# MLA head loop: the next head's first key/value tile (T0) multiplied ahead of the key transposes (kp) instead of behind them

## The chip, the cores and the metric

The kernel runs on one core of a Trainium2 chip. The metric is the device time of one execution in microseconds. A profiled execution of the kernel before took 2205.33 us; the trace of it spans 2203.3 us.

## The reference

One inference step of a two-layer encoder: a forgetting-attention layer (FoX), then a multi-head latent attention layer (MLA), for a prompt of 512 tokens and for 64 new tokens that follow 512 cached ones. The change lies in the MLA attention. With c the normalised latent (512 wide) of all tokens and w_ukv its up-projection, each of 16 heads computes

```
kv     = c @ w_ukv[head]                        # 256 wide: 128 key columns, 128 value columns
kn, v  = rms_norm(kv[:, :128]) * g_kn, kv[:, 128:]
logits = (qn @ kn.T + qr @ kr.T) * MLA_SCALE    # nope part + rotary part (kr shared by the heads)
p      = softmax(where(kpos // 64 <= qpos // 64, logits, -1e30))
o      = (p @ v) * silu(gate)
```

and then y = x + o @ w_out. Everything is fp32. The kernel splits each operand of a matmul into a rounded high part and a low part (fp32r) and adds three products, hi*hi, hi*lo and lo*hi.

## The kernel before

The MLA attention is `block_f` (line 2514), with the helpers of class `MlaHead`. It is one software pipeline over heads: one pass of the loop does the attention of head g = h - 1 and, between its steps, the key/value projection of head h. Passes run for h = 0 (no g), h = 1 to 14 as seven turns of a hardware loop with two passes each, h = 15, and at last one with g = 15 alone, in which the output projection takes the place of the tiles.

The order of a pass is a list of names written out by hand, `ORDER` (line 2109). Each of the engines walks the same list and emits what that name means for it; all waits are semaphores between engines. An engine's queue is in order, so an instruction that waits holds all behind it. The names:

- **T0 to T7**: TensorE multiplies one tile of 128 tokens with the head's weights (`pe_tile`, line 2251): 12 matmuls of 256 columns, two tiles to a PSUM bank, banks 0 to 3. T0 to T3 are prompt tokens, T4 to T7 cached ones. T8 (8 matmuls, bank 4) is for the new tokens. T0 waits for the head's split weights and, in `v_lo`, until VectorE has taken the values of the head before out of bank 0. After T1, T3, T5 and T7 ScalarE squares the keys of the two tiles (`act_keys`), VectorE turns the sums into variances (`dve_sums`), GpSimd takes the root, and VectorE writes the normalised keys to f_k (`dve_keys`) in two halves: the first (prompt keys) at the name "sb" of the same pass, the second (cached and new keys) at "kp" of the next.
- **kp, ka, new**: TensorE transposes the prompt keys, the cached keys, and the new tokens' queries and keys (`pe_job`, line 2276). ScalarE copies the result to the high part and VectorE subtracts to get the low part (f_kphi, f_kplo; f_knhi, f_knlo).
- **s3 to s0, sa, sb**: scores of four prompt blocks (s3 is the longest, 512 columns) and of the new tokens. VectorE masks and takes the maximum (f_nm), ScalarE the exponential (f_p; f_pn for the new tokens).
- **p3 to p0, pn**: transposes of the probabilities, split as above (f_pt3hi, f_pt3lo, ...). **on, o**: probabilities times values. **g**: transposes of the gate, which VectorE has scaled by the reciprocal of the softmax sum (`dve_scale_gate`). **ont**: transpose of the new tokens' output. **qr, qn**: transposes of the next head's queries, split into f_qr, f_qnhi and f_qnlo.

The jobs (names without T) take turns in three PSUM banks, 5, 6 and 7, in the order of the list. So `wait_operands` (line 2202) makes each job wait until the third job before it has been taken out of its bank, besides its own inputs: kp shares its bank with qn, s2, s0, p3, p1 and g; s3 with o and new; p1 waits for f_pt3lo. s3 to s0 need kp, qr and qn to be split, sa and sb need ka and new.

At the name "kp" the other engines do more than the job. ScalarE, after f_kphi, waits for the second half of the keys, takes the values out of banks 2, 3 and 4 (f_v_past) and rounds the next head's weights (f_whi). VectorE, after f_kplo, writes the second half of the keys and then the values' low parts. The names T0, T2 and T6 mean nothing to them. `FIRST`, the order of the pass h = 0, is made from `ORDER`; `FINAL`, the order of the last pass, is a list of its own.

GpSimd, besides the roots, does leftovers of the stage before in the first passes (scaling and rotating the queries of the last heads, e_q and e_rt) and parts of the output projection's splits in the last. SP issues the loads: the next queries once "new" has run, the next gate once "ont" has run.

Of the kernel before, what the change touches and what calls it, by code (L numbers as in the profile page):

```python
# [2101 lines left out]
class MlaHead:  # L2102
# [3 lines left out]

    ORDER = ["kp", "T0", "T1", "s3", "ka", "T2", "s2", "new", "T3", "s1", "s0", "T8", "sa", "sb", "T4",
             "p3", "T5", "pn", "p2", "p1", "T6", "on", "p0", "g", "T7", "ont", "qr", "qn", "o"]  # L2110
    NEXT = ("qr", "qn")
    FIRST = [n for a in ORDER if a not in ("qr", "qn") for n in ((a, "qr", "qn") if a == "T5" else (a,))]
    FINAL = ["kp", (0, 0), (0, 1), "s3", "ka", (0, 2), "s2", "new", (0, 3), "s1", "s0", (0, 4), "sa", "sb", (1, 0), (1, 1),
# [3 lines left out]
    SPLIT_AT = {"T2": 0, "T3": 1, "T7": 2, (0, 1): 3, (1, 3): 4, (2, 3): 5, (3, 3): 6}  # L2117
    JOBS = [n for n in ORDER if n[0] != "T"]
    SPLITS = ["kp", "ka", "new", "p3", "pn", "p2", "p1", "p0", "qr", "qn"]
# [64 lines left out]
    def order(self, h):  # L2184
        return self.FINAL if h is None else self.FIRST if isinstance(h, int) and h == 0 else self.ORDER

# [709 lines left out]
```

How the kernel before makes its waits and increments, by code:

```python
    def wait(self, eng, step, k):  # L70
        v = (step * self.per + k + self.credit + self.ahead) * self.unit
        if not isinstance(v, int) or v > 0:
            eng.wait_ge(self.sem, v)
# [186 lines left out]
    def pe(self, eng, part=slice(None)):  # L261
        for i, b, ks, s, prev in self.jobs()[part]:
            if prev is not None:
                eng.wait_ge(self.lo_out.sem, prev + 1)
            for j, k in enumerate(ks):
                if s:
                    op = eng.transpose(self.c.bank[b][:, j * NEW:(j + 1) * NEW],
                                       self.src[0:NEW, SM, k * P:(k + 1) * P], self.ident[0:NEW, 0:NEW])
                else:
                    for t in range(NT):
                        op = eng.transpose(self.c.bank[b][:, t * P:(t + 1) * P],
                                           self.src[:, t, k * P:(k + 1) * P], self.ident[:, :])
            op.then_inc(self.turned.sem, 1)
# [1 line left out]
    def act(self, eng, part=slice(None)):  # L275
        for i, b, ks, s, _ in self.jobs()[part]:
            src, hi, lo = self.views(b, ks, s)
            eng.wait_ge(self.turned.sem, i + 1)
            eng.activation(hi, src, ACT.Copy).then_inc(self.hi_out.sem, 1)
# [1 line left out]
    def dve(self, eng, part=slice(None)):  # L281
        for i, b, ks, s, _ in self.jobs()[part]:
            src, hi, lo = self.views(b, ks, s)
            eng.wait_ge(self.hi_out.sem, i + 1)
            eng.tensor_tensor(lo, src, hi.bitcast(F32), ALU.subtract).then_inc(self.lo_out.sem, 1)
```

## Time and profile before

| | |
|---|---|
| median of 3 runs | 2205.38 us (2205.34 to 2206.18) |
| profiled execution, its time | 2205.33 us |
| its span in the trace | 2203.3 us |
| TensorE, matmul / weight load | 99% / 85% of the span |
| VectorE, ScalarE, GpSimd | 51%, 43%, 10% |
| MLA head loop, passes with kp and tiles | 1612.2 to 1985.3 us, 15 passes |
| a steady pass | 24.77 us |

Line 2270 is the tiles' matmul, 2299 the transposes of kp and ka, 2305 and 2307 the scores, 2328 the product o, 2337 the gate's transposes. A row of a timeline has the start in us, the duration in us, the engine (PE is TensorE's matmul, PEld its weight load, DVE VectorE, ACT ScalarE, POOL GpSimd), the line, the operation, output<-inputs, sizes, how many are merged, and in brackets the idle time of that engine just before it and what ended it. Matmuls overlap in the trace: the next one starts while the record of the one before is still open, so the time that one takes of the stream is the distance between starts.

### The profile page before, as it was taken

The page shows a single profiled execution, that of the slowest core. Times are in us where ns is not written, and L with a number is a line of the kernel's source. Part 1 is how long each engine was busy: PE and PEld are TensorE (multiplying, and loading weights), DVE is VectorE, ACT ScalarE, POOL GpSimd, SP SyncE. Part 2 cuts the span into 40 slices and gives each one's busy share as a digit, 9 for nine tenths or more (in the row PEclk, how much of TensorE's full clock was granted, in tenths as well). Part 3 has the DMA queues.
Part 4 walks back from the last instruction along what each step waited for, and adds up shares of the span by engine and source line. Part 5 has one row for each costly group of instructions (what it writes and reads, how often), then busy time and mean ns, then how long its engine had stood idle before and what let it go on. Part 6 is the DMA issues. An engine that isn't in the chain of part 4 may idle for free. (4 is left out here: it accounts for less than half of the span.)

```text
span 2203.3 us, 33500 instructions
## 1 busy us (share of the span) xinstructions
PE 2187.6 (99%) x11665; PEld 1872.6 (85%) x11665; DVE 1119.6 (51%) x2676; ACT 955.7 (43%) x2242; POOL 229.5 (10%) x248
## 2 busy tenths in 40 slices
PE   9999999999999999999999999999999999999999
PEld 6888888888888888888888988888899999998887
DVE  6645554445454545555223344454477777775232
ACT  5444444434444444453223433344366666664111
POOL 0100000000000000000000001332150100021000
PEclk9999999999999999999999999999999999999999
DMA  5333332333333334333432332433431212122542
GB/s 180 104 102 111 101 101 92 106 106 101 98 90 103 110 101 101 102 103 115 156 119 82 108 103 80 148 115 133 129 103 48 60 51 57 48 60 71 172 128 92
DMA packets 127443, 225.27 MB, mean 102 GB/s; under 512 B 21216, under 2 KB 70624, under 8 KB 127248
## 3 DMA queue, kind: packets, MB, share of 16 engines
q1 hardware_dynamic: 127376, 224.36, 33.2%
q8 instruction: 45, 0.74, 0.1%
q14 instruction: 22, 0.18, 0.0%
HBM read 191.42 MB, written 32.89 MB: 102 GB/s over the span
## 5 line engine op out<-in xcount | busy, mean ns | idle before, releaser
L213 PE MATMUL bank<-b_whi,x_hi 128*128 128x512 f32 x1016 | 401.8, 395 | 0.8 <-DVE b_wlo L196 0.8
L213 PE MATMUL bank<-b_whi,x_lo 128*128 128x512 f32 x1016 | 396.5, 390 | 0.0
L213 PE MATMUL bank<-b_wlo,x_hi 128*128 128x512 f32 x1016 | 396.5, 390 | 0.0
L196 DVE SCALAR_TENSOR_TENSOR b_wlo<-b_raw,g_fox,b_whi 128x512 fp32r<-128x512 f32 x254 | 179.1, 746 | 137.4 <-ACT b_whi L183 136.9
L183 ACT ACTIVATE b_whi<-b_raw,g_fox 128x512 fp32r<-128x512 f32 x254 | 169.1, 714 | 152.7 <-PE bank L213 134.8
L213 PEld LDWEIGHTS bank<-b_whi,x_lo 128*128 128x128 f32 x1016 | 190.7, 188 | 41.0
L213 PEld LDWEIGHTS bank<-b_whi,x_hi 128*128 128x128 f32 x1016 | 190.9, 188 | 37.3 <-DVE b_wlo L196 1.1
L213 PEld LDWEIGHTS bank<-b_wlo,x_hi 128*128 128x128 f32 x1016 | 190.9, 188 | 35.3
L213 PE MATMUL bank<-m_whi,x_hi 128*128 128x512 f32 x320 | 125.0, 391 | 0.0
L213 PE MATMUL bank<-m_wlo,x_hi 128*128 128x512 f32 x320 | 124.6, 389 | 0.0
L213 PE MATMUL bank<-m_whi,x_lo 128*128 128x512 f32 x320 | 124.6, 389 | 0.0
L196 DVE SCALAR_TENSOR_TENSOR m_wlo<-m_raw,g_mla,m_whi 128x512 fp32r<-128x512 f32 x80 | 61.7, 812 | 95.7 <-ACT m_whi L183 95.6
L183 ACT ACTIVATE m_whi<-m_raw,g_mla 128x512 fp32r<-128x512 f32 x80 | 53.4, 716 | 124.8 <-PE bank L213 124.8
L1048 POOL TENSOR_TENSOR b_decay<-b_decay,mask_fox 128x128 f32<-128x128 f32 x64 | 27.8, 466 | 738.1 <-DMA b_decay_new<-decay 738.1
L213 PE MATMUL bank<-c_whi,x_hi 128*128 128x512 f32 x256 | 100.7, 393 | 1.2 <-DVE x L1445 1.2
L213 PE MATMUL bank<-b_whi,x_smp 128*128 128x512 f32 x254 | 101.8, 401 | 0.0
L213 PE MATMUL bank<-g_whi,g_ohi 128*128 128x512 f32 x256 | 100.4, 392 | 0.0
L213 PE MATMUL bank<-c_whi,x_lo 128*128 128x512 f32 x256 | 99.8, 390 | 0.0
L213 PE MATMUL bank<-c_wlo,x_hi 128*128 128x512 f32 x256 | 99.7, 390 | 0.0
L213 PE MATMUL bank<-g_whi,g_olo 128*128 128x512 f32 x256 | 99.7, 389 | 0.0
L213 PE MATMUL bank<-g_wlo,g_ohi 128*128 128x512 f32 x256 | 99.7, 389 | 0.0
L192 DVE TENSOR_TENSOR g_wlo<-g_raw,g_whi 128x1024 fp32r<-128x1024 f32 x32 | 39.1, 1223 | 118.9 <-ACT g_whi L179 118.9
(506 smaller groups left out, 5102.2 us busy)
## 6 DMA issues: line engine op xcount, KB each, us to landing
b_raw<-w_fox SPq DMA_DIRECT2D x127, 512.0 KB, 3.5
m_raw<-w_mla SPq DMA_DIRECT2D x40, 512.0 KB, 3.5
c_raw<-w_out SPq DMA_DIRECT2D x32, 512.0 KB, 3.5
g_raw<-w_out SPq DMA_DIRECT2D x32, 512.0 KB, 3.5
f_raw<-w_ukv SPq DMA_DIRECT2D x16, 512.0 KB, 3.6
queries<-e_q SPq DMA_DIRECT2D x16, 480.0 KB, 3.8
e_raw<-w_uq SPq DMA_DIRECT2D x32, 192.0 KB, 2.6
f_qa<-queries SPq DMA_DIRECT2D x16, 320.0 KB, 3.7
```

The lines of the kernel that those rows point to most:

```text
L183: op = eng.activation(hi[:, k, :], raw[:, k, :], ACT.Copy, scale=self.gain[:, K:K + 1])
L192: op = eng.tensor_tensor(lo[:], raw[:], hi32, ALU.subtract)
L196: op = eng.scalar_tensor_tensor(lo[:, k, :], raw[:, k, :], self.gain[:, K:K + 1], hi32[:, k, :], ALU.mult, ALU.subtract)
L213: op = eng.matmul(out, a, w[:, k, :], start=(first and k == 0 and i == 0), stop=(last and k == self.kk - 1 and i == len(pairs) - 1))
L1048: pool.tensor_tensor(x, x, K.mask_fox[:], ALU.add).then_inc(H.decay_masked.sem, 1)
```

## The change

In `ORDER` the first two names change places. The list is read by all engines, but only TensorE does something at T0, so only its order changes: the 12 matmuls of T0 stand ahead of the four transposes of kp in each pass with a g and an h. `FIRST` is derived from `ORDER` (in the pass h = 0 kp does nothing on TensorE), `FINAL` stays. Which bank each job uses, and what it waits for, is unchanged.

```diff
-    ORDER = ["kp", "T0", "T1", "s3", "ka", "T2", "s2", "new", "T3", "s1", "s0", "T8", "sa", "sb", "T4",
+    ORDER = ["T0", "kp", "T1", "s3", "ka", "T2", "s2", "new", "T3", "s1", "s0", "T8", "sa", "sb", "T4",
              "p3", "T5", "pn", "p2", "p1", "T6", "on", "p0", "g", "T7", "ont", "qr", "qn", "o"]
```

## Rows read from the trace of the kernel before

**Rows 1.** By windows: span, busy time (count) of each engine, PEclk, DMA.
```profile
1711.74:1736.51 24.77, 24.52 (x190) 23.02 (x190) 18.11 (x60) 15.22 (x56) 2.17 (x2) 1.00 0.18 53
...
1959.31:1985.27 25.96, 24.95 (x190) 23.04 (x190) 19.50 (x60) 18.19 (x62) 10.12 (x10) 1.00 0.27 80
```
**Rows 2.** Waits of TensorE: us in total, times, longest.
```profile
PE bank L2299 <- DVE f_qnlo L2438: 3.6, 15, 0.3
```
**Rows 3.** Timeline of TensorE, a steady pass, from o to new.
```profile
1711.21 0.27 PE L2328 MATMUL bank<-f_pt3hi,f_v_own 128*128 128x128 f32 x1
1711.74 0.65 PE L2299 MATMUL bank<-ident,f_k 128*128 128x128 f32 x4 [0.26 <-DVE f_qnlo L2438]
1712.15 0.36 PE L2270 MATMUL bank<-f_whi,c_hi 128*128 128x256 f32 x1
...
1715.11 0.40 PE L2305 MATMUL bank<-f_kphi,f_qnhi 128*128 128x512 f32 x1
...
1716.27 0.60 PE L2299 MATMUL bank<-ident,f_k 128*128 128x128 f32 x4
...
1719.10 0.43 PE L84 MATMUL bank<-ident,f_qa 64*128 64x64 f32 x2
```
**Rows 4.** Timeline of VectorE, the same pass.
```profile
1710.92 0.69 DVE L2438 TENSOR_TENSOR f_qnlo<-bank,f_qnhi 128x512 fp32r<-128x512 f32 x1
...
1713.06 0.69 DVE L2438 TENSOR_TENSOR f_kplo<-bank,f_kphi 128x512 fp32r<-128x512 f32 x1 [0.65 <-ACT f_kphi L2358]
...
1716.16 0.27 DVE L2511 TENSOR_TENSOR f_v_past<-f_kv_new,f_v_past 64x128 fp32r<-64x128 f32 x1
```
**Rows 5.** Timeline of ScalarE, the same pass.
```profile
1712.43 0.60 ACT L2358 ACTIVATE f_kphi<-bank 128x512 fp32r<-128x512 f32 x1 [1.81 <-PE bank L2299]
1715.07 0.66 ACT L2429 ACTIVATE f_v_past<-bank 128x256 fp32r<-128x256 f32 x2 [2.04 <-DVE f_k L2505]
...
1717.38 0.69 ACT L2383 ACTIVATE f_p<-bank,f_nm 128x512 f32<-128x512 f32 x1
...
1725.66 0.50 ACT L2378 ACTIVATE f_pn<-bank,f_nm 64x288 f32<-64x288 f32 x1 [0.77 <-DVE f_nm L2449]
```
**Rows 6.** Timelines of VectorE and TensorE, the same pass, from s1 to g.
```profile
1721.96 0.11 DVE L2453 MEMSET bank<- 64x64 f32 x1 [0.23 <-PE bank L2307]
...
1727.82 0.29 DVE L2438 TENSOR_TENSOR f_pt3lo<-bank,f_pt3hi 128x128 fp32r<-128x128 f32 x1 [0.49 <-ACT f_pt3hi L2358]
...
1728.47 0.36 PE L2270 MATMUL bank<-f_whi,pc_hi 128*128 128x256 f32 x1
...
1729.97 1.05 DVE L2486 TENSOR_SCALAR f_gate<-f_gate,f_ri 128x128 f32<-128x128 f32 x5
...
1731.14 0.42 PEld L2337 LDWEIGHTS bank<-ident,f_gate 128*128 128x128 f32 x4 [0.19 <-issue]
```
**Rows 7.** Timelines of all engines in the first pass with kp.
```profile
1611.99 0.74 DVE L2511 TENSOR_TENSOR f_v_own<-bank,f_v_own 128x256 fp32r<-128x256 f32 x2
...
1612.20 0.65 PE L2299 MATMUL bank<-ident,f_k 128*128 128x128 f32 x4 [0.16 <-DVE f_qnlo L2438]
...
1615.35 2.41 POOL L1761 TENSOR_TENSOR e_q<-e_raw,e_rstd 128x1280 f32<-128x1280 f32 x1
1617.84 4.44 POOL L1769 TENSOR_TENSOR e_rt<-e_raw,e_tab 128x320 f32<-128x320 f32 x4
...
1616.69 1.21 DVE L2511 TENSOR_TENSOR f_v_past<-f_kv_new,f_v_past 64x128 fp32r<-64x128 f32 x1
...
1618.79 0.69 ACT L2383 ACTIVATE f_p<-bank,f_nm 128x512 f32<-128x512 f32 x1 [0.89 <-DVE f_nm L2455]
...
1626.60 0.50 ACT L2378 ACTIVATE f_pn<-bank,f_nm 64x288 f32<-64x288 f32 x1 [0.93 <-DVE f_nm L2449]
...
1628.77 0.29 DVE L2438 TENSOR_TENSOR f_pt3lo<-bank,f_pt3hi 128x128 fp32r<-128x128 f32 x1 [0.49 <-ACT f_pt3hi L2358]
...
1629.41 0.36 PE L2270 MATMUL bank<-f_whi,pc_hi 128*128 128x256 f32 x1
```

## The prediction

> **What bounds the kernel now.** I read the view by windows first. One steady pass of the MLA head loop, from one set of key transposes ("kp") to the next, lasts 24.77 us; TensorE is busy for 24.52 of them and its granted clock is 1.00 [rows 1]. That looks like a TensorE bound with nothing to win or lose. It isn't one: matmuls are pipelined, so busy time hides where the array stood still. The list of waits shows one wait in every pass: kp waits for VectorE's low half of the query split, 15 times, 0.3 us at most [rows 2]. The timelines of one pass then show a second loop, as long as TensorE's own. It runs through ScalarE and VectorE and touches TensorE at few places:
>
> kp transposes -> ScalarE copies them (f_kphi, 1712.43) -> VectorE subtracts (f_kplo, 1713.06) and scales the second half of the keys -> ScalarE takes values (f_v_past waited 2.04 us for those keys), the next weights and two squares -> exponential of score row s3 at 1717.38 -> split of ka -> maxima and exponentials of the other rows -> exponential of the sample rows (f_pn) at 1725.66 -> split of p3 -> TensorE's p1 transposes and T6 -> VectorE scales the gate -> TensorE's "g" transposes [rows 3 to 6].
>
> The last two steps touch TensorE with no slack. The p3 subtraction ends at 1728.11, and p1 takes over its bank; the T6 matmul behind p1 starts at 1728.47. The gate scaling ends at 1729.97 + 1.05 = 1731.02, and g's first weight load is at 1731.14 after 0.19 us without work [rows 6]. So TensorE is already paced by this chain at p1 and g, and whatever delays kp delays them, unless the chain has slack in between.
>
> **What is removed.** T0 needs nothing that is late: its weights and its bank were freed in the pass before, so it can start right behind "o". The last product of o starts at 1711.21; a matmul of 256 columns takes 0.12 of the stream (below) and this one of 128 a little less, so T0 could start at 1711.32. It now starts at 1712.15, behind a kp that waited for f_qnlo (1710.92 + 0.69 = 1711.61) and started at 1711.74 [rows 3, 4]. From kp's start to T0's are 0.41 here; in a full stream it is 0.05 less, as its four transposes then last 0.60 (ka's row) and not 0.65. 1711.32 + 0.36 = 1711.68 is where T0 would come without the wait; the wait costs 1712.15 - 1711.68 = 0.47 us of TensorE a pass. In the new order the query split is long done when kp comes. No instruction or DMA is added or taken away, and no other queue has its order changed: ScalarE and VectorE do nothing for T0. SP issues the next query's loads after "new", some 0.1 us later than now, and they are used at the end of the pass, at qr and qn.
>
> **What is moved.** 24 matmuls of T0 and T1 and one restart lie between 1712.15 and 1715.11, so a matmul takes about 0.12 us and T0 1.44 to 1.49 (I take 1.46). kp then starts at 1711.32 + 1.46 = 1712.78 instead of 1711.74, 1.04 later. Its transposes last 0.60 instead of 0.65, so f_kphi starts 1.0 later, at 1713.43. f_kplo follows at 1714.06 and ends at 1714.75.
>
> Near TensorE this costs little. T1 with its restart is the other 1.50 of the 2.96, so s3 would start at 1712.78 + 0.36 + 1.50 = 1714.64; it has to wait for f_kplo plus a hop of 0.13 (as from f_qnlo's end to kp), so 1714.88, still 0.23 ahead of 1715.11. ka needs the scaled keys, which come 1.0 later, at about 1716.04 (f_v_past starts on them at 1715.07 now): start 1716.17 against 1716.27. "new" needs the exponential of s3, which then begins at 1718.38 and lasts 0.69, so with the hop new starts no earlier than 1719.20, against 1719.10: now behind [rows 3, 5]. All of that is overruled further on.
>
> **Slack in the chain.** From f_kphi to the exponential of s3 (4.95 us) every step waits for the one before; TensorE is not in it, so the delay of 1.0 arrives whole. Between the exponential of s3 and f_pn the steady pass takes 1725.66 - 1717.38 = 8.28 us. Of this, 0.23 is VectorE waiting for TensorE's s1 ahead of a MEMSET [rows 5, 6]; other waits for TensorE are too short to be marked. The first pass of the loop shows what the stretch takes when the chain runs late and never waits for TensorE: there the exponential was at 1618.79 and f_pn at 1626.60, 7.81 us [rows 7]. So 0.47 of the delay is absorbed and 0.53 arrives at f_pn. Behind it nothing gives: f_pt3lo ends 2.45 us after f_pn starts in the steady pass and 2.46 in the first, and T6 follows that end by 0.36 and 0.35 [rows 6, 7]. p1, g, T7, the gate's users and o are all moved by 0.53, and the next T0 with them.
>
> The cycle closes: 24.77 + 0.53 = 25.30 us. The wait of 0.47 that goes is not subtracted from this, since TensorE isn't what closes the cycle any more: it stands at s3, ka, new and p1 instead. If the chain didn't close the cycle, the gain would be the 0.47.
>
> **The sum.** kp is in 15 passes. 13 of them are steady: 13 x 0.53 = 6.9. In the first pass T0 also has to wait for VectorE's first f_v_own, about half of the pair at 1611.99 (1612.37 + 0.13 = 1612.50), so kp comes at 1613.96 instead of 1612.20, and this pass has no slack left: 1.71 at most. But it also has a VectorE subtraction on the chain that took 1.21 us, beside a GpSimd operation that ran from 1615.35 to 1617.76; shifted to 1618.4 it falls on the middle of the next one (four of 1.11 each from 1617.84), so it waits for some 0.5 instead of 0.94 [rows 7]. I take 1.3, with 0.8 and 1.71 as ends. In the last pass (1959.31 to 1985.27, already 25.96 long, [rows 1]) the output projection's splits of o stand in ScalarE's queue; I take 0.8, between 0.5 (as in a steady pass) and 1.0 (nothing absorbed). Sum 6.9 + 1.3 + 0.8 = 9.0. The profiled execution took 2205.33 us, the median of the runs is 2205.38, so nothing is to be corrected: 2205.3 + 9.0 = 2214.3 us. For the unknown: the steady pass from 0.45 (T0 at 1.44, hops a little shorter) to 0.67 (the 0.24 of slack that no row marks only half there); with the ends of the other two 7.2 to 11.4, so 2212.5 to 2216.7.
>
> The Trainium skill (Perfetto Trace Analysis, Optimization Strategy) says to look for gaps on the engine that should be saturated, find the semaphore behind each, and make that dependency start sooner. That is this change, taken at the gap before kp; by it alone the result is rival 1. The Trainium skill also says (SBUF — State Buffer, SBUF: two separate sides) that a VectorE operation with two SBUF inputs and a GpSimd operation that reads SBUF lock one pair of ports against each other for their whole length. The 1.21 us subtraction is such a form, and it takes 0.27 us in a steady pass [rows 4], so the trace agrees; by it the first pass could end anywhere between my two ends.
>
> **Rivals.**
> 1. *The gap simply closes.* 15 x 0.47 = 7.1 us less: 2198.2. For it: the wait is there in 15 passes, TensorE reads as busy everywhere, T0 is ready. Against it: g waits 0.19 us in the passes now, which it wouldn't if the chain had room, and p1 follows f_pt3lo as closely in both kinds of pass. It needs 1.0 us of slack between f_kphi and f_pt3lo; I found 0.47.
> 2. *The delay ends at the near waits.* If p1 has more room than the rows tell, TensorE keeps what "new" leaves it, 0.1 to 0.2 behind: 15 x 0.15 = 2.3, so 2207.6; and if even new isn't held, ka's 0.1 ahead gives 15 x 0.1 = 1.5 less, 2203.8. Either is within 0.2% of before. For it: several of these links sit within 0.1 us of each other. Against it: the first pass.
> 3. *Nothing is absorbed.* 13 x 1.0 + 1.7 + 1.0 = 15.7: 2221. It would need VectorE's 0.23 and the unmarked 0.24 to stay waits for TensorE, though TensorE is delayed less than they are. Against it: the first pass again.
>
> **Chances.** Forecast 0.72; rival 1 0.07; rival 2 0.11; rival 3 0.05; 0.05 for what I have not seen (on the slow side by half). What a measurement can tell from no change is 0.2%, 4.4 us, so faster is below 2201.0 and slower above 2209.8: faster 0.07, same 0.10, slower 0.83. The range takes the forecast's own bounds, widened towards rivals 2 and 3: 2209.5 to 2218.
>
> **What the changed kernel's profile would show.** The wait of kp for f_qnlo is gone and T0 starts 0.1 us behind o. The pass lasts 25.3 us. f_kphi starts about 2.2 us after o's last product started instead of 1.22. TensorE now waits at s3 for f_kplo (0.2), at ka for f_k, at new for f_p and, largest, at p1 for f_pt3lo (0.2 to 0.5); g's wait stays about as it is. From the exponential of s3 to f_pn 7.8 us instead of 8.28. I am wrong if the pass is at or under 24.77, or if p1 doesn't wait; then the chain had slack where I saw none. The granted clock stays at 1.00: no stop is longer than those it has now.

## The result: 9.1 us slower, and the profile after

| | before | changed |
|---|---|---|
| median of the runs | 2205.36 us (2205.04 to 2206.18, 6 runs) | 2214.49 us (2213.99 to 2215.29, 6 runs) |
| ratio of the medians | 1 | 1.0042, 95% interval 1.0030 to 1.0053 |
| profiled execution, span | 2205.33 us, 2203.3 us | 2214.54 us, 2212.5 us |
| one steady pass, first product of o to the next | 24.76 us | 25.24 us |

The forecast was 2214.3 us. On every engine the changed kernel runs the same instructions in the same order as before; only TensorE's order differs.

One steady pass by windows, from kp to kp, with the columns of [rows 1]:

```profile
1716.43:1741.67 25.24, 25.10 (x192) 23.04 (x191) 17.95 (x59) 14.82 (x56) 2.17 (x2) 1.00 0.19 54
```

TensorE reads busier than before in that pass (25.10 of 25.24 against 24.52 of 24.77) although it does the same work in more time. Busy time shows nothing of the cause. The list of waits does. TensorE's weight loads in the stretch of the head loop (1600 to 2020 us), columns as in [rows 2], first the kernel before and then the changed one (L2299 is kp and ka, L84 new, L2337 g):

```profile
PEld bank L2299 <- issue: 5.4, 14, 0.4
PEld bank L84 <- issue: 4.2, 16, 0.4
PEld bank L2337 <- issue: 2.6, 14, 0.2
```

```profile
PEld bank L84 <- ACT f_p L2383: 6.6, 16, 0.8
PEld bank L2305 <- issue: 3.8, 15, 0.3
PEld bank L2322 <- DVE f_pt3lo L2438: 3.6, 15, 0.3
PEld bank L2337 <- issue: 2.9, 15, 0.2
...
PEld bank L2299 <- DVE f_k L2505: 2.0, 7, 0.7
PEld bank L2270 <- DVE f_v_own L2511: 0.7, 1, 0.7
...
PEld bank L2299 <- DVE f_qnlo L2438: 0.3, 1, 0.3
```

The query split as releaser of kp's line is down to one short wait in the whole loop (15 waits in [rows 2]). In its place TensorE stops at five places in every pass: at s3 (L2305, 0.26), at ka (L2299), at the transposes "new" (L84, 0.41, where it was some 0.26 before), at p1 (L2322, 0.23) and still at g (L2337, 0.20). TensorE's timeline and its weight loads, the steady pass that answers to [rows 3]:

```profile
1714.84 0.27 PE L2328 MATMUL bank<-f_pt3hi,f_v_own 128*128 128x128 f32 x1
1714.95 0.33 PE L2270 MATMUL bank<-f_whi,c_hi 128*128 128x256 f32 x1
...
1716.43 0.60 PE L2299 MATMUL bank<-ident,f_k 128*128 128x128 f32 x4
...
1718.52 0.49 PE L2305 MATMUL bank<-f_kphi,f_qnhi 128*128 128x512 f32 x1
```
```profile
1718.51 0.19 PEld L2305 LDWEIGHTS bank<-f_kphi,f_qnhi 128*128 128x128 f32 x1 [0.26 <-issue]
1719.72 0.42 PEld L2299 LDWEIGHTS bank<-ident,f_k 128*128 128x128 f32 x4 [0.22 <-DVE f_k L2505]
...
1722.78 0.29 PEld L84 LDWEIGHTS bank<-ident,f_qa 64*128 64x128 f32 x2 [0.41 <-ACT f_p L2383]
...
1732.27 0.31 PEld L2322 LDWEIGHTS bank<-ident,f_p 128*128 128x128 f32 x3 [0.23 <-DVE f_pt3lo L2438]
```

T0 starts 0.11 us behind o's last product. kp comes 1.59 behind that product, where it came 0.53 behind it. ScalarE and VectorE in the same pass, for [rows 4 to 6]:

```profile
1717.06 0.60 ACT L2358 ACTIVATE f_kphi<-bank 128x512 fp32r<-128x512 f32 x1 [2.82 <-PE bank L2299]
1719.70 0.66 ACT L2429 ACTIVATE f_v_past<-bank 128x256 fp32r<-128x256 f32 x2 [2.04 <-DVE f_k L2505]
1721.95 0.69 ACT L2383 ACTIVATE f_p<-bank,f_nm 128x512 f32<-128x512 f32 x1
...
1729.76 0.50 ACT L2378 ACTIVATE f_pn<-bank,f_nm 64x288 f32<-64x288 f32 x1 [0.93 <-DVE f_nm L2449]
```
```profile
1726.31 0.11 DVE L2453 MEMSET bank<- 64x64 f32 x1
...
1731.92 0.29 DVE L2438 TENSOR_TENSOR f_pt3lo<-bank,f_pt3hi 128x128 fp32r<-128x128 f32 x1 [0.48 <-ACT f_pt3hi L2358]
```

f_kphi starts 2.22 us behind o's last product; that was 1.22. The exponential of s3 is followed by f_pn after 7.81 us (8.28 before), and VectorE's MEMSET has lost its wait of 0.23 for TensorE's s1.

**Where the 9.1 us are.** The start of o's first product in each pass gives the books:

| stretch | before | changed | difference | forecast |
|---|---|---|---|---|
| VectorE's first f_wlo of the loop to o of pass 1 | 30.40 | 32.37 | +1.97 | +1.3 (0.8 to 1.71) |
| o of pass 1 to o of pass 2 | 24.76 | 25.56 | +0.80 | +0.53 |
| 12 passes to o of pass 14 | 297.16 | 302.92 | +5.76 (0.48 each) | 12 x 0.53 |
| o of pass 14 to kp of the last order | 28.25 | 28.92 | +0.67 | +0.8 |
| work ahead of the loop | | | -0.11 | 0 |

Sum 9.1. The 12 steady passes were put 0.6 too large and the last one 0.1, the first two too small by 0.94. That the sum came out within 0.1 is luck.

### The profile page after: what moved, and what is told of

It reads as the page before. It is cut to its first block and busy times, and to the rows that moved or that the text cites. A ratio compares the mean times of both kernels' runs of the same rounds, so it can differ in the third digit from the quotient of the medians.

```text
span 2212.5 us, 33500 instructions
## 1 busy us (share of the span) xinstructions
PE 2197.1 (99%) x11665; PEld 1873.1 (85%) x11665; DVE 1117.2 (50%) x2676; ACT 950.9 (43%) x2242; POOL 229.6 (10%) x248
## 5 line engine op out<-in xcount | busy, mean ns | idle before, releaser
L213 PE MATMUL bank<-b_whi,x_hi 128*128 128x512 f32 x1016 | 401.8, 395 | 0.8 <-DVE b_wlo L196 0.8
L213 PE MATMUL bank<-b_wlo,x_hi 128*128 128x512 f32 x1016 | 396.5, 390 | 0.0
L213 PE MATMUL bank<-b_whi,x_lo 128*128 128x512 f32 x1016 | 396.4, 390 | 0.0
L213 PEld LDWEIGHTS bank<-b_whi,x_lo 128*128 128x128 f32 x1016 | 190.7, 188 | 41.0
L213 PEld LDWEIGHTS bank<-b_whi,x_hi 128*128 128x128 f32 x1016 | 190.9, 188 | 37.2 <-DVE b_wlo L196 1.0
L213 PEld LDWEIGHTS bank<-b_wlo,x_hi 128*128 128x128 f32 x1016 | 191.0, 188 | 35.3
L213 PE MATMUL bank<-m_whi,x_hi 128*128 128x512 f32 x320 | 125.0, 391 | 0.0
L213 PE MATMUL bank<-m_wlo,x_hi 128*128 128x512 f32 x320 | 124.6, 389 | 0.0
L213 PE MATMUL bank<-m_whi,x_lo 128*128 128x512 f32 x320 | 124.6, 389 | 0.0
L213 PE MATMUL bank<-c_whi,x_hi 128*128 128x512 f32 x256 | 100.7, 393 | 1.2 <-DVE x L1445 1.2
L213 PE MATMUL bank<-b_whi,x_smp 128*128 128x512 f32 x254 | 101.8, 401 | 0.0
L213 PE MATMUL bank<-g_whi,g_ohi 128*128 128x512 f32 x256 | 100.5, 393 | 0.0
L213 PE MATMUL bank<-c_whi,x_lo 128*128 128x512 f32 x256 | 99.8, 390 | 0.0
L213 PE MATMUL bank<-c_wlo,x_hi 128*128 128x512 f32 x256 | 99.7, 390 | 0.0
L213 PE MATMUL bank<-g_whi,g_olo 128*128 128x512 f32 x256 | 99.7, 390 | 0.0
L213 PE MATMUL bank<-g_wlo,g_ohi 128*128 128x512 f32 x256 | 99.7, 389 | 0.0
L213 PE MATMUL bank<-b_wlo,x_smp 128*128 128x512 f32 x254 | 99.3, 391 | 0.0
```

The lines of the kernel that those rows point to most:

```text
L213: op = eng.matmul(out, a, w[:, k, :], start=(first and k == 0 and i == 0), stop=(last and k == self.kk - 1 and i == len(pairs) - 1))
```

## The experiments

Where an experiment cuts T0 in two, the line numbers lie 3 higher than before (2 higher in the two kernels with GpSimd's work cut). Each time stands beside runs of the kernel before on the same chip. "Chain" is the second loop that the prediction describes, through ScalarE and VectorE from kp to p1 and g; "stream" is TensorE's own work with what it waits for at kp.

**Part of T0 ahead of kp.** The cleanest test is the dose. If the chain closes the pass, every matmul ahead of kp costs its 0.12 us; if the stream does, the first few that fill the wait gain.

```
ORDER = ["T0a", "kp", "T0b", "T1", "s3", ...]      # T0a: the first 3 (6, 9) of T0's 12 matmuls
if part == "a" and 3 * k + i >= AHEAD_OF_KP or part == "b" and 3 * k + i < AHEAD_OF_KP: continue
```

> The kernel before, with the first 3 of T0's 12 matmuls ahead of kp and the other 9 behind it. They take 0.41 us of TensorE, about the gap, so kp starts where it did (0.53 us behind the start of o's last product) and f_kphi with it. Theory, two loops: a pass ends when the later of two arrives at f_pn, TensorE's own stream (14.45 us behind o's last product in the kernel before) or the chain through ScalarE and VectorE (1.22 + 4.95 + 7.81 = 13.98 us), and 10.32 us follow in either case. Here the stream comes 0.39 earlier and the chain is as before, so a pass takes 24.38 us, 15 x 0.39 = 5.9 us less in all: 2199.5. Rival A, one loop: the chain alone closes the cycle in the kernel before already, as g's wait for the gate shows; filling the gap gives nothing: 2205.3, a pass of 24.77. Rival B, near waits (what cost time in the changed kernel are the waits right behind kp, at s3 for f_kplo and at ka for f_k): there are none here, so 2199.5 as well.

Measured: 2202.50 us (before 2204.91; ratio 0.9989, interval 0.9980 to 0.9998), steady pass 24.43.

> The kernel before, with 9 of T0's 12 matmuls ahead of kp. kp starts 0.7 us later than before, f_kphi 0.66 later. s3 and ka should come without a wait: f_kplo would end at 1714.4 on the clock of the pass before and s3 start at 1714.65, the keys at 1715.7 and ka at 1715.8. Theory, two loops: the chain arrives at f_pn after 13.98 + 0.66 = 14.64 us against 14.45 before, so a pass takes 24.96 us, 15 x 0.19 = 2.9 us more: 2208.2, though neither s3 nor ka waits; p1 waits for f_pt3lo. Rival A, one loop: nothing is absorbed, 15 x 0.66 = 9.9 more: 2215. Rival B, near waits: none are left and the gap is gone, 15 x 0.4 less: 2199.4.

Measured: 2209.38 us (before 2204.91; ratio 1.0020, 1.0011 to 1.0029), steady pass 24.87.

> The kernel before with 6 of T0's 12 matmuls ahead of kp. So far 0, 3, 9 and 12 ahead gave steady passes of 24.77, 24.43, 24.87 and 25.25 us. Theory, two loops: from the point at which the chain becomes the longer loop on, each matmul ahead of kp costs its 0.12 us; from the 24.87 with 9 ahead back by 3 x 0.12 that is 24.51 us, nearly the 24.43 of 3 ahead. Rival (a cost that grows with each of the 12 and a gain that is there once kp's wait is covered): 0.42 gained, less half of 0.9 lost: 24.80.

Measured: 2205.02 us in one run (before 2205.42), steady pass 24.53.

| matmuls of T0 ahead of kp | 0 | 3 | 6 | 9 | 12 |
|---|---|---|---|---|---|
| steady pass, us (the passes of a run agree within 0.03) | 24.77 | 24.43 | 24.53 | 24.87 | 25.24 |

From 6 to 12 a matmul costs 0.12 us a pass, its whole time in the stream. Drawn on to 3 that line would give 24.17; the pass is 24.43, where the stream ends it, 0.34 below before. So there are two bounds, and they cross between 3 and 6 matmuls. The waits at p1 agree. Here are TensorE's waits in the head loop with 3 ahead (first fence) and with 9 ahead (second); p1 is L2325, g is L2340, new is L84:

```profile
PEld bank L84 <- issue: 4.0, 15, 0.4
PEld bank L2340 <- issue: 2.7, 14, 0.2
...
PEld bank L2325 <- DVE f_pt3lo L2441: 0.8, 3, 0.3
```
```profile
PEld bank L84 <- ACT f_p L2386: 6.3, 16, 0.8
PEld bank L2325 <- DVE f_pt3lo L2441: 3.4, 15, 0.3
PEld bank L2340 <- issue: 2.9, 15, 0.2
```

With 3 ahead p1 waits in 3 passes, with 9 in all 15, although with 9 no steady pass has a wait at s3. So the wait at s3 isn't the cause of the loss. At ka TensorE still waits 0.2 to 0.3 in the steady passes with 9 ahead, though the expectation was that it wouldn't; this run alone doesn't clear ka, the late copies below do. The total of the run with 3 ahead missed its expectation by 3 us, that with 9 by 1.2. With 3 ahead the steady passes were 24.43 where 24.38 was expected, which is 0.7 of the miss; the first pass was as long as the changed kernel's (32.37 us from f_wlo to o), which is most of the rest. That opened the question of the first pass (below).

**The chain shortened.** In the changed kernel, work that stands in the chain but isn't needed by it is moved behind: ScalarE's rounding of the next weights from kp to ka, VectorE's low parts of the values behind s3's maximum and those of the weights to s2.

```
-  if name == "kp" and not last: H.act_weights(act_, h + 1, 1 - par)
+  if name == "ka" and not last: H.act_weights(act_, h + 1, 1 - par)
-  (at kp, behind dve_keys)      for b in (2, 3, 4): H.dve_values(dve, g, b, 1 - par)
+  (at s3, behind its maximum)   for b in (2, 3, 4): H.dve_values(dve, g, b, 1 - par)
-  if name == "s3" and not last: H.dve_weights(...)
+  if name == "s2" and not last: H.dve_weights(...)
```

> The changed kernel (T0 ahead of kp), with the work that stands between kp and the exponential of s3 moved out of that stretch: ScalarE rounds the next weights behind ka's split instead of behind f_v_past, VectorE writes f_v_past's low parts behind s3's maximum instead of ahead of it and the weights' low part behind s2's maximum. Nothing is left out and TensorE's order is that of the changed kernel. Theory, two loops: the exponential of s3 comes some 0.8 to 0.9 earlier, the chain reaches f_pn after about 14.2 us, and TensorE's stream (which still waits at s3 and ka, 0.1 ahead of the kernel before) sets it at 14.35: a pass of 24.67 us instead of 25.25, so 8 to 9 us less than the changed kernel: about 2205.5, the changed kernel's loss is gone. new and p1 wait no more. Rival A, one loop: the pass falls by the whole 0.9 that the chain loses: 2201. Rival B, near waits: s3's and ka's waits stay as they are, so the loss stays: at least 2212. Rival C (the loss comes from TensorE's own stream, by the way the 12 matmuls and the transposes follow each other): 2214.5 as the changed kernel.

Measured: 2207.89 us (before 2204.91; ratio 1.0015, 1.0006 to 1.0024), steady pass 24.66 to 24.71. The pass fell as expected, the total is 2.4 us above the expected 2205.5. The same moves in the kernel before:

> The kernel before with the same two moves that shortened the path behind the exponential of s3 in the changed kernel (ScalarE's rounding of the next weights from kp to ka, VectorE's low parts of the values to behind s3's maximum and those of the weights to s2). My theory: before the change the path through the two other engines isn't what ends last in the steady pass (0.47 us of slack), so shortening it gives nothing: 24.77 us a pass, p1 and new without a wait as before, 2205.4 us, or 0.5 us more because the last pass's tail now waits for f_v_past, as it did in the changed kernel. The rival (the path always bounded the pass): 24.2 us a pass and 2198.

Measured: 2207.57 us (before 2205.21; ratio 1.0010, 1.0001 to 1.0020), steady pass 24.77. The steady pass didn't move, so before the change the chain was not what closed it. The exponential of s3 starts 6.17 us behind o's last product with the moves and without them: ScalarE now waits 0.96 for s3's maximum there, and VectorE waited 1.48 for TensorE's s3. In the kernel before, TensorE's path to that exponential and the one through ScalarE's queue are equally long. One pass of it with the moves:

```profile
1715.67 0.11 DVE L2453 MEMSET bank<- 64x64 f32 x1 [1.48 <-PE bank L2307]
...
1716.55 0.69 ACT L2383 ACTIVATE f_p<-bank,f_nm 128x512 f32<-128x512 f32 x1 [0.96 <-DVE f_nm L2455]
```

The total missed: it is 2.4 us up, because in the last pass TensorE now waits 2.2 us for VectorE's values (L213 below), a price of the moves and not of the order of T0. TensorE's waits in the changed kernel with the short chain, and then in the kernel before with it:

```profile
PEld bank L2305 <- issue: 3.8, 15, 0.3
...
PEld bank L213 <- DVE f_v_past L2511: 2.2, 1, 2.2
PEld bank L2299 <- DVE f_k L2505: 2.0, 7, 0.7
...
PEld bank L2322 <- DVE f_pt3lo L2438: 0.3, 1, 0.3
```
```profile
PEld bank L213 <- DVE f_v_past L2511: 2.2, 1, 2.2
...
PEld bank L2322 <- DVE f_pt3lo L2438: 0.3, 1, 0.3
```

Against its own before the first is up by 2.98 us and the second by 2.36. With this chain the order of T0 therefore costs 0.6 us instead of 9.1, which the intervals don't tell from nothing. Part of it is TensorE's clock. In the profiled run of the kernel before with the short chain the granted clock falls to 0.50 (1.2 of 2.4 GHz) 0.8 us behind the end of the stop of 2.24 us, while the changed kernel has the same stop and keeps 1.00 (columns as in [rows 1]):

```profile
1992.30:1995.60 3.30, 3.30 (x11) 2.57 (x10) 0.84 (x4) 0.00 (x0) 1.62 (x2) 0.50 0.41 146
```
```profile
1992.00:1996.00 4.00, 3.70 (x18) 3.00 (x19) 2.46 (x6) 1.09 (x4) 2.77 (x3) 1.00 0.37 131
```

From the first product of o in pass 15 to that of the last pass it is 36.07 us there and 34.52 here, 32.31 without the moves. Of the 10 runs of the kernel before with the short chain, the five with a mean clock of 1.0 took 2206.60 to 2207.18 us, the others 2207.97 to 2209.76; of the 11 of the changed kernel three are below 1.0. Runs at 1.0 alone give 1.8 and 2.8 us against before, so 1.0 for the order. In the loop it costs 1.1 in the first pass (31.01 against 29.92) and gains 0.06 to 0.11 in a steady one, 1.0 in 12. What stays of the gap of 0.47 seems to go to the near waits at s3 and ka, which haven't changed; no run takes those away alone. That is the prediction's rival 2, and it shows up once the chain is out of the way.

**ScalarE's copies of the values later.** ScalarE makes two copies (f_v_own) in the chain's stretch between f_pn and the split of p3. VectorE needs them only for their low parts, behind the gate, and TensorE only in o, so they can stand behind the split of p1. From f_pn's start to f_pt3lo's end a steady pass then takes 1.90 us and not 2.45.

```
   (at "sb", behind f_pn)
-  H.keys.wait(act_, h, 1)
-  for b in (0, 1): H.act_values(act_, h, b, par)
   (at "p1", behind its split)
+  H.keys.wait(act_, h, 1)
+  for b in (0, 1): H.act_values(act_, h, b, par)
```

> The changed kernel (T0 ahead of kp), in which ScalarE copies the values of banks 0 and 1 (0.66 us) behind the split of p1 instead of at sb. Nothing ahead of f_pn is touched: kp comes as late as in the changed kernel, and s3, ka and new wait as there. Theory, two loops with the ScalarE-VectorE chain as the longer one in the changed kernel: 0.44 us of the chain between f_pn and the gate go, so a pass takes 25.25 - 0.44 = 24.81 us and the whole 15 x 0.44 = 6.6 us less than the changed kernel, about 2207.8. Rival, near waits (s3, ka and new hold TensorE and set the time): they stay, only p1's and g's waits of 0.2 each can go; if they are in series with the near ones that gives the same 0.4, if the near ones set the pace it gives nothing: 2214.5. Rival, TensorE's own stream: 2214.5.

Measured on the changed kernel: 2209.34 us (before 2205.42; ratio 1.0018, 1.0009 to 1.0027), steady pass 24.90 where 24.81 was expected.

> The kernel before with ScalarE's two copies of the new values (f_v_own) moved from ahead of the weights of the smp tile to behind the high part of p1: what the best version so far has, without the three matmuls ahead of the key transposes. My theory: in the kernel before TensorE's stream bounds the steady pass from s3 on, with 0.47 us stopped at kp, and the copies in their old place cost 0.15 to 0.25 us a pass (g's wait). So the steady pass takes 24.55 to 24.65 us, kp's wait of 0.47 stays, and the kernel takes 2202.5 us. Rival: the copies' gain needs a stream with no wait at kp, or the wait at kp grows by what is saved: 24.77 a pass and 2205.4.

Measured on the kernel before: 2203.49 us (before 2205.21; ratio 0.9993, 0.9983 to 1.0002, so the total alone doesn't tell it from no change), steady pass 24.64.

> Kernel e1_t0_3_ahead, and in it ScalarE copies the values of banks 0 and 1 (f_v_own, 0.66 us) behind the split of p1 instead of at sb, between the exponentials of the new tokens and the split of p3. That shortens the chain from f_pn to p1 and g by 0.44 (then VectorE's own work is the longer of the two). Theory, two loops: p1's and g's waits (0.05 and 0.2) go and nothing else: a pass of 24.38 - 0.24 = 24.14 us, 15 x 0.63 = 9.4 us less than before: 2196. Rival A, one loop: the chain loses 0.44 and the gap gives nothing: 15 x 0.44 = 6.6 less: 2198.7. Should e1 show no gain, this shows whether the stretch behind f_pn is what holds it.

Measured with 3 matmuls of T0 ahead: 2197.69 us (before 2204.91; ratio 0.9967, 0.9955 to 0.9979), steady pass 24.27 where 24.14 was expected.

The changed kernel gains 0.34 a pass, from a move that touches neither kp, s3, ka nor new. Its near waits are as they were, but for a longer one at ka in the first pass; p1's and g's are gone (TensorE's waits in the changed kernel with late copies):

```profile
PEld bank L84 <- ACT f_p L2383: 6.7, 16, 0.8
PEld bank L2305 <- issue: 3.8, 15, 0.3
PEld bank L2299 <- DVE f_k L2505: 2.7, 7, 1.4
```

This is the most direct evidence that the loss came through p1 and g. That a pass still takes 24.90, against 24.64 with the same copies in the kernel before, is by the list the near waits, which stay. The kernel before gains only 0.13, because its stream bounds the pass; what goes there is g's wait of 0.2 (L2337 isn't among its waits any more). With 3 ahead both bounds fall: 24.64 - 24.27 = 0.37 from closing the gap at kp, and 0.50 below before in all. The total owes 2 us to the first pass, which is back at 30.39 (32.37 with 3 ahead alone), for the reason told in the last section. This is the best version found.

**The first pass.** In the changed kernel T0, and kp behind it, waits there 0.73 us for VectorE's f_v_own. First I took away that wait, by writing these low parts earlier in the pass h = 0:

```
-  if name == "p1":
+  if name == ("T5" if g is None else "p1"):
       for b in (0, 1): H.dve_values(dve, h, b, par)
```

> The changed kernel; in the pass h = 0 alone VectorE writes the low parts of f_v_own at T5, where it idles for 2.17 us, instead of at p1, behind f_qnlo. T0 of the first pass with kp waited for them (to 1612.35). Theory: it starts when T7 is through, about 0.55 us earlier, and kp with it; the first pass gives back some 0.5 us of the 1.96 us that it cost, less or more as VectorE's subtractions then meet GpSimd's operations. Steady passes stay at 25.25. Rival (that wait is covered by something else, kp's wait for f_qnlo or the keys): no change in the first pass.

Measured: 2214.51 us in one run; kp did come sooner (1613.22 instead of 1613.87), and the first pass lasted 32.37 us from f_wlo to o, as without the edit. The expected 0.5 us weren't there. The timeline of VectorE shows why: the gain went into one operation. The changed kernel's first pass, then that of this experiment:

```profile
1616.78 0.82 DVE L2505 SCALAR_TENSOR_TENSOR f_k<-f_kv_new,f_rstd,g_kn 64x128 f32<-64x128 f32 x1
...
1618.72 0.67 DVE L2511 TENSOR_TENSOR f_v_past<-f_kv_new,f_v_past 64x128 fp32r<-64x128 f32 x1
...
1620.16 1.88 DVE L2417 TENSOR_TENSOR f_wlo<-f_raw,f_whi 128x1024 fp32r<-128x1024 f32 x1
```
```profile
1616.13 1.58 DVE L2505 SCALAR_TENSOR_TENSOR f_k<-f_kv_new,f_rstd,g_kn 64x128 f32<-64x128 f32 x1
...
1618.84 0.67 DVE L2511 TENSOR_TENSOR f_v_past<-f_kv_new,f_v_past 64x128 fp32r<-64x128 f32 x1
...
1620.27 1.88 DVE L2417 TENSOR_TENSOR f_wlo<-f_raw,f_whi 128x1024 fp32r<-128x1024 f32 x1
```

0.65 sooner, 0.76 longer. GpSimd was in one operation, the scaling of a group of queries, from 1615.13 to 1617.46 in the changed kernel and 0.11 later with the edit. So GpSimd was the suspect, and the next pair cuts its work in both kernels to a few columns, which leaves most of the last two groups of queries uncomputed:

```
+  n = 8 if g >= 6 else HD
-  pool.tensor_tensor(flat(q[:])[:, :, 0:HD], v[:, :, 0:HD], wide_to(e_rstd[:, 0:M], HD), ALU.mult)
+  pool.tensor_tensor(flat(q[:])[:, :, 0:n], v[:, :, 0:n], wide_to(e_rstd[:, 0:M], n), ALU.mult)
   (the four e_rt and two e_q operations behind it likewise, 2 of 32 columns)
```

> The kernel before, with GpSimd's last two groups of queries (those that it works on beside the first two passes of the loop over heads) cut to a few columns: the multiplies e_q<-e_raw,e_rstd and e_rt<-e_raw,e_tab and the two sums behind them do 8 and 2 columns instead of 128 and 32, so the queries of these groups are left mostly uncomputed. This pair (with the next run) tests whether the first passes are long because VectorE's operations with both inputs in SBUF are stretched beside GpSimd's. My theory: in the first pass f_v_past<-f_kv_new takes 0.3 us instead of 1.21, the subtraction f_wlo 1.2; the first product of o starts 0.2 to 0.6 us sooner than 1635.10, and the whole kernel is 0.3 to 0.6 us faster (2204.8). The rival (the stretch has another cause, as a DMA or ScalarE): the durations stay and so does the time, 2205.4.

Measured: 2205.03 us (before 2205.21; ratio 0.9999, 0.9989 to 1.0008).

> The changed kernel with the same cut. My theory: f_k<-f_kv_new takes 0.33 us instead of 0.82, f_v_past 0.27 instead of 0.67, f_wlo 1.2 instead of 1.88; the first product of o in the first pass starts 0.8 to 1.0 us sooner than 1636.96, the second pass takes 25.25 instead of 25.56 us, steady passes stay at 25.25, and the kernel takes 2213.3 us. The difference between this pair is then 8.2 to 8.5 us, against 9.1 between the uncut kernels. The rival: the same durations, first product at 1636.96, 2214.5 and a difference of 9.1.

Measured: 2213.15 us (ratio 1.0035, 1.0021 to 1.0050). VectorE in the first pass of the pair, before and then changed:

```profile
1614.56 0.34 DVE L2507 SCALAR_TENSOR_TENSOR f_k<-f_kv_new,f_rstd,g_kn 64x128 f32<-64x128 f32 x1
...
1616.02 0.27 DVE L2513 TENSOR_TENSOR f_v_past<-f_kv_new,f_v_past 64x128 fp32r<-64x128 f32 x1
...
1617.12 1.22 DVE L2419 TENSOR_TENSOR f_wlo<-f_raw,f_whi 128x1024 fp32r<-128x1024 f32 x1
```
```profile
1617.55 0.33 DVE L2507 SCALAR_TENSOR_TENSOR f_k<-f_kv_new,f_rstd,g_kn 64x128 f32<-64x128 f32 x1
...
1619.01 0.27 DVE L2513 TENSOR_TENSOR f_v_past<-f_kv_new,f_v_past 64x128 fp32r<-64x128 f32 x1
...
1620.05 1.21 DVE L2419 TENSOR_TENSOR f_wlo<-f_raw,f_whi 128x1024 fp32r<-128x1024 f32 x1
```

All three operations have their short time in both kernels. GpSimd's work is the cause of the stretch; the work of ScalarE and of the DMAs was left as it was.

| first f_wlo to o of pass 1 | GpSimd as it is | cut | GpSimd's share |
|---|---|---|---|
| before | 30.40 | 29.93 | 0.47 |
| changed | 32.37 | 31.09 | 1.28 |
| difference | 1.97 | 1.16 | 0.81 |

The second pass of the changed kernel went from 25.56 to 25.23, the steady ones stayed (25.23, and 24.77 before). The pair is 2213.15 - 2205.03 = 8.1 us apart against 9.1; 8.2 to 8.5 was expected. GpSimd's share of the changed kernel's first pass, 1.28 counted from f_wlo, is above the 0.8 to 1.0 expected. The kernel before gained 0.47 in the loop, and its median fell by 0.18; its interval reaches from 2.4 below to 1.8 above, so its total tells neither.

**The best version with the first pass's edit** (3 matmuls ahead, late copies but not in the pass h = 0, and the edit above):

> e4_3_ahead_late_values (3 matmuls of T0 ahead of kp, values of banks 0 and 1 copied behind p1's split), and the values of the pass h = 0 taken early on both engines as in e7_after_first_pass. Theory: steady passes as in e4, 24.27 us, where TensorE waits for nothing but the far end of its own stream; the first pass 0.3 to 0.8 us shorter. 2197.2, against 2197.7 for e4 and 2204.9 for the kernel before. If the first pass's GpSimd work sets it instead, 2197.7.

Measured: 2199.92 us (2197.56 to 2201.29; before 2205.42; ratio 0.9974, 0.9964 to 0.9984), steady pass 24.27, first pass 30.32 against 30.39 without the edit. The expectation was 2197.2. It gains nothing over the version without it, which was 7.2 us below its own before where this is 5.5. The profiled execution took 2198.04 us, near the lowest run, so the trace doesn't show what the others lost; that is open.

## Why the prediction was right, point by point

- **What is removed.** Held: kp no longer waits for the query split, T0 starts 0.11 behind o, and no other engine's order changed. That the 0.47 is not subtracted from the pass held too.
- **What is moved.** kp came 1.06 later behind o (1.04 forecast), f_kphi 1.00 (1.0 forecast), s3 waits 0.26 (0.23), new and ka wait as told. The largest wait was told for p1; it is 0.23 there and 0.41 at new.
- **Slack in the chain.** This was the step that carried the sign, and the exact number held: 7.81 us from s3's exponential to f_pn, so 0.47 absorbed. The pass grew by 0.48 and not 0.53; between f_kphi and s3's exponential the changed kernel takes 4.89 where the kernel before took 4.95 (ScalarE's stretch from f_v_past on), and that is the difference. That TensorE isn't in that stretch is true of the changed kernel only: in the kernel before, the way through TensorE's s3 was as long. The dose, the short chain and the late copies each show the chain's closing of the pass separately.
- **First pass.** The term was 1.3 and measured 1.97, outside its ends of 0.8 and 1.71; the second pass, counted as steady, measured 0.80. Counted from VectorE's first f_wlo, kp came 1.78 later (1.76 forecast) and f_kphi 1.73. What failed is "so it waits for some 0.5 instead of 0.94": I shifted the one subtraction that was long before (f_v_past) and left the others as they were. In the changed kernel that one did get shorter, 0.67 instead of 1.21, but f_k, which took 0.33 before (it started at 1615.24, ahead of GpSimd's operation of [rows 7]), moved into it and took 0.82. So the stretch from f_kphi to the exponential of s3 gave back 0.13 (5.77 against 5.90) and not 0.44. And f_wlo took 1.88 instead of 1.22, so the exponential of s3 is followed by f_pn after 8.18 and not 7.81: 1.73 - 0.13 + 0.37 = 1.97. The ends should have come from shifting every operation of VectorE in that stretch. That "this pass has no slack left" was GpSimd's doing too. With its work cut f_pn follows the exponential after 8.29 before and 7.80 changed, as in a steady pass, and the first pass costs 1.16. The Trainium skill (SBUF — State Buffer, SBUF: two separate sides) says that a VectorE operation with two SBUF inputs and a GpSimd operation that reads SBUF lock each other out for their whole length. The pair of experiments agrees: 0.82 against 0.33, 1.88 against 1.21.
- **Last pass.** 0.8 forecast, 0.67 measured.
- **Rivals.** That the gap simply closes would have been 2198.2; the run with 3 matmuls ahead shows how much of it can be had with the chain as it is, 0.34 of 0.47 a pass. The near waits are real but decide only with the chain shortened or its copies moved. That nothing is absorbed was excluded by the 7.81.

Open: what the near waits at s3 and ka cost by themselves, and why the version with the first pass's edit varies by 3.7 us from run to run.

## What to carry to other kernels

An engine at 99% busy with one marked wait can still be one of two loops of equal length. Before filling that wait, follow the work that the filler pushes back (here the transposes that feed ScalarE and VectorE) to the next place where it comes back to the engine, and compare its slack with the delay; if the slack is smaller, fill the wait only with as much as the slack bears (3 matmuls of 12 here), and look for work inside the other loop that isn't needed by it. Where the loop runs beside a third engine for some of its passes, shift every operation against that engine's, not only the one that was long before.

## What was unexpected of the hardware

- VectorE's f_k, 0.33 us with its operands in SBUF, took 0.82 (changed kernel), 1.58 (first pass's edit), 1.89 and 1.99 us (3 and 6 matmuls ahead) where it began inside GpSimd's operation of 2.33 us. In all four it ended 0.06 us after GpSimd's next operation had started, however much sooner it had begun. Its end went by GpSimd's, and coming 0.65 us sooner bought nothing. In the kernel before, f_k began 0.11 us ahead of GpSimd's operation and took 0.33; there GpSimd's took 2.41 instead of 2.33 [rows 7]. With 3 ahead and late copies it was again 0.11 ahead and took 0.34, and that first pass is 2 us shorter than with 3 ahead alone. Which of the two starts first decides, here for up to 1.6 us; no run has it start less than 0.4 us behind GpSimd's.
- The stretch goes both ways: GpSimd's sum e_q<-e_rt, 0.87 us in the kernel before, took 1.75 in the first pass of the changed kernel, beside the long f_wlo:

```profile
1615.13 2.33 POOL L1761 TENSOR_TENSOR e_q<-e_raw,e_rstd 128x1280 f32<-128x1280 f32 x1
1617.54 3.42 POOL L1769 TENSOR_TENSOR e_rt<-e_raw,e_tab 128x320 f32<-128x320 f32 x4
1621.03 1.75 POOL L1773 TENSOR_TENSOR e_q<-e_rt 128x320 f32<-128x320 f32 x1
```
- A stop of 2.24 us of TensorE in the last pass, the same in both kernels with the short chain, was followed by 3.3 us at a granted clock of 0.50 in one profiled run and by none in the other. The mean clock was below 1.0 in 5 of 10 and in 3 of 11 of their runs, and in none of the runs of the unchanged kernel before.
